# The last layer norm of a three-block transformer with tokens on partitions, its result transposed before it is scaled

## What is computed

```python
x = layer_norm(ALPHA * x + merged @ w_out[l], ln1_g[l], ln1_b[l])
u = causal_dwconv(x @ w_up[l], f_conv_w[l], f_conv_b[l])
u_gate, u_val = jnp.split(u, 2, -1)
x = layer_norm(ALPHA * x + (jax.nn.silu(u_gate) * u_val) @ w_down[l], ln2_g[l], ln2_b[l])
# layer_norm(x, g, b): (x - mean) * rsqrt(var + 1e-5) * g + b, over the 1024 features
```

## Time and profile before

| what | us |
|---|---|
| median of 3 runs (2580.94 to 2585.09) | 2582.67 |
| the profiled execution | 2586.92 |
| its span | 2585.1 |
| TensorE busy in it | 2513.1 |
| mean granted TensorE clock, share of full speed | 0.988 |

### The profile page before, as it was taken

The page is one execution under the profiler, slowest core; times in us unless marked ns, Lnnn a source line. Parts: engine busy times, 40 slices in busy tenths (PEclk is TensorE's granted clock), DMA queues, the critical chain, the costliest instruction groups (busy, mean ns, idle before and its releaser), DMA issues.

```text
span 2585.1 us, 30721 instructions
## 1 busy us (share of the span) xinstructions
PE 2513.1 (97%) x11112; PEld 1990.6 (77%) x11112; DVE 1369.7 (53%) x1916; ACT 667.3 (26%) x1101; POOL 1563.8 (60%) x1061
## 2 busy tenths in 40 slices
PE   7999999999999999999999999999999999999998
PEld 6875688888877776688867886867888777888876
DVE  5975683221379999968214426344356244534534
ACT  3006621100254434421022114133114121300102
POOL 2640257766779898667643765624764467666653
PEclk8999999999999999999999999999999999999999
DMA  9620132333222322122321231311332222233321
GB/s 298 222 94 1 52 123 86 98 98 98 98 82 82 97 73 74 53 98 96 105 76 33 98 98 46 103 49 53 98 94 66 65 82 93 70 98 98 89 96 47
DMA packets 224141, 231.46 MB, mean 90 GB/s; under 512 B 12219, under 2 KB 213788, under 8 KB 223900
## 3 DMA queue, kind: packets, MB, share of 16 engines
q1 hardware_dynamic: 221104, 229.33, 28.0%
q10 hardware_dynamic: 2924, 0.66, 0.1%
HBM read 227.87 MB, written 2.10 MB: 89 GB/s over the span
## 4 chain that ended last, share of the span: by engine, by line
PE 85%; DVE 8%; DVEq 2%; ACT 2%; POOLq 1%; issue 1%; POOL 1%; DMA 1%; ACTq 0%; SPq 0%
PE PS L1540 64%; PE PS L1487 7%; DVE PS L3076 3%; PE PS L1348 3%; PE PS L2136 1%; DVEq L3078 1%; PE PS L1007 1%; PE PS L2338 1%; PE PS L2355 1%; PE PS L2127 1%; DVE PS L3120 1%; PE PS L2723 1%; DMA spare<-in_ada_w 1%; POOLq L1457 1%; PE PS L1777 0%
## 5 line engine op out<-in xcount | busy, mean ns | idle before, releaser
L1461 POOL TENSOR_TENSOR Wl<-raw,Wh 128x512 fp32r<-128x512 f32 (+1 forms) x764 | 1035.2, 1386 | 28.1 <-issue 0.5
L1455 POOL TENSOR_SCALAR Wh<-raw 128x2048 fp32r<-128x2048 f32 (+1 forms) x195 | 367.6, 1886 | 808.9 <-issue 370.9
L1540 PE MATMUL PS<-Hh,Wh 128*128 128x512 f32 x1936 | 765.9, 396 | 29.3 <-POOL Wl L1461 20.9
L1540 PE MATMUL PS<-Hl,Wh 128*128 128x512 f32 x1936 | 758.7, 392 | 0.0
L1540 PE MATMUL PS<-Hh,Wl 128*128 128x512 f32 x1936 | 758.5, 392 | 0.0
L1540 PEld LDWEIGHTS PS<-Hh,Wh 128*128 128x128 f32 x1936 | 366.5, 189 | 116.0 <-POOL Wl L1461 20.3
L1540 PEld LDWEIGHTS PS<-Hl,Wh 128*128 128x128 f32 x1936 | 366.8, 189 | 78.0 <-issue 1.9
L1540 PEld LDWEIGHTS PS<-Hh,Wl 128*128 128x128 f32 x1936 | 366.3, 189 | 77.5
L1540 PE MATMUL PS<-Bh,Wh 128*128 128x512 f32 x640 | 249.4, 390 | 2.1 <-POOL Wl L1461 2.1
L1540 PE MATMUL PS<-Bh,Wl 128*128 128x512 f32 x640 | 249.0, 389 | 0.0
L1540 PE MATMUL PS<-Bl,Wh 128*128 128x512 f32 x640 | 249.0, 389 | 0.0
(11 more groups left out here) (497 smaller groups left out, 3091.7 us busy)
## 6 DMA issues: line engine op xcount, KB each, us to landing
raw<-in_w_in SPq DMA_DIRECT2D x44, 1024.0 KB, 5.4
raw<-in_w_ff SPq DMA_DIRECT2D x32, 1024.0 KB, 5.3
raw<-in_conv_w_in SPq DMA_DIRECT2D x24, 1024.0 KB, 5.2
raw<-in_ret_w_in SPq DMA_DIRECT2D x24, 1024.0 KB, 5.1
spare<-in_ada_w SPq DMA_DIRECT2D x20, 1024.0 KB, 8.9
raw<-in_w_up SPq DMA_DIRECT2D x20, 1024.0 KB, 5.3
raw<-in_w_out SPq DMA_DIRECT2D x8, 1024.0 KB, 4.9
raw<-in_conv_w_out SPq DMA_DIRECT2D x8, 1024.0 KB, 5.0
```

The source lines that it names most:

```text
L1455: pool.tensor_scalar(st.Wh[0:rows, slot, k, 0:cols], st.raw_slot(slot)[0:rows, k, 0:cols], 1.0, 1.0, ALU.mult, ALU.mult)
L1461: ins = pool.tensor_tensor(st.Wl[0:rows, slot, k, 0:cols], st.raw_slot(slot)[0:rows, k, 0:cols], st.Wh[0:rows, slot, k, 0:cols].bitcast(F3 ...
L1540: mm = pe.matmul(out, lhs, rhs, start=(k == parts[0][0] and n == 0), stop=(k == parts[-1][0] and n == 2))
```

## The change

`CentredNorm` for ln2 and `store_part` are replaced by one class, `LastNorm`. In short:

- **During down 2** (now one round of four phases): behind chunk k=3 of tile 2, TensorE transposes X chunks 0 to 3 as they are into banks 4 to 7. Tile 3 is multiplied one bank after the other (all of b=0, then all of b=1), with transposes of chunks 4, 5 in the first half and 6 in the second. VectorE takes `bn_stats` of these banks, which have tokens on partitions, so that a statistic is one number for each partition. It adds chunk 6 to X after the first bank.
- **After down 2:** chunk 7 is added, transposed and counted; `bn_aggr` gives mean and variance for each token; ScalarE has meanwhile made gain x X for each chunk (`scaled`), and TensorE turns these into banks of the result. The mean and the bias come into the same banks by one product for each bank: `spread` (columns with the mean and the standard deviation in high and low parts) times `factors` (rows with gain and bias). VectorE and ScalarE multiply by rstd on the way from PSUM, and four stores follow, one for each 128 tokens.
- **Between down 0 and up 1** stands a new part, `prepare`: VectorE clears the rows and the columns, SP waits for this and loads gain and bias as six rows (two DMAs of 12 KB), and VectorE rounds and splits them.
- The 18 small products before the transposes, the pivot and the sums of squares are gone.

```diff
+    def load_rows(self, sp):
+        sp.wait_ge(self.cleared, 1)
+        sp.dma_start(self.rows[0:3, :], self.gain_row.to_broadcast([3, D])).then_inc(self.rows_in, 16)
+        sp.dma_start(self.rows[3:6, :], self.bias_row.to_broadcast([3, D])).then_inc(self.rows_in, 16)
+
+    def make_rows(self, dve):
+        dve.wait_ge(*self.rows_free)
+        dve.memset(self.rows, 0.0)
+        dve.memset(self.columns.bitcast(F32), 0.0)
+        dve.tensor_tensor(self.low_row, self.st.ident[:, 1:2], self.st.ident[:, 4:5], ALU.add)
+        dve.drain().then_inc(self.cleared, 1)
+        dve.tensor_scalar(self.sign, self.low_row, -2.0, 1.0, ALU.mult, ALU.add)
+        dve.wait_ge(self.rows_in, 32)
+        dve.tensor_copy(self.rounded, self.rows)
+        dve.drain()
+        dve.tensor_scalar(self.rows, self.rows, self.low_row, None, ALU.mult)
+        dve.drain()
+        dve.scalar_tensor_tensor(self.factors, self.rounded.bitcast(F32), self.sign, self.rows, ALU.mult,
+                                 ALU.add).then_inc(self.rows_made, 1)
...
+    def within_bank(self, pe, p, b, k):
+        if (p, b, k) == (2, 0, 3):
+            self.raw(pe, (0, 1, 2, 3))
+        if (p, b, k) == (3, 0, 3):
+            self.raw(pe, (4, 5))
+        if (p, b, k) == (3, 1, 3):
+            self.raw(pe, (6,))
...
+    def counts_before_last(self, dve, i, p):
+        self.count(dve, 0)
+        dve.wait_ge(self.first_bank, 1)
+        self.add(dve, self.st.PS[:, 2 * self.own_slot(), :], 6).then_inc(self.seventh_in, 1)
+        self.count(dve, 1)
+        self.count(dve, 2)
...
+        pe.wait_ge(self.counted, NB)
+        turn_scaled(0, 0)
+        self.raw(pe, (7,))
+        for b in range(1, NB):
+            turn_scaled(b, 0)
+        pe.wait_ge(self.counted, 3 * NB)
+        for b in range(2):
+            turn_scaled(b, 1)
+        pe.wait_ge(self.columns_in, 1)
+        spread = st.PS[:, self.bank(3, 1), :]
+        for b in range(NB):
+            mm = pe.transpose(spread[:, b * P:(b + 1) * P], self.columns[:, b, :].bitcast(F32), st.ident)
+        mm.then_inc(self.columns_turned, 1)
+        turn_scaled(2, 1)
+        pe.wait_ge(self.rows_made, 1)
+        pe.wait_ge(self.columns_copied, 1)
+        add_means(0, 0)
+        add_means(0, 1)
+        turn_scaled(3, 1)
+        for b in range(1, NB):
+            add_means(b, 0)
+            add_means(b, 1)
...
+    def vector(self, dve):
+        st = self.st
+        self.count(dve, 3)
+        dve.drain()
+        for b in range(NB):
+            dve.bn_aggr(self.moments[:, b, :], self.counts[:, b, :, :].rearrange("p g n -> p (g n)"))
+        dve.drain().then_inc(self.var_in, 1)
+        dve.tensor_scalar(self.pair[:, :, 0], self.moments[:, :, 0], -1.0, None, ALU.mult)
+        dve.wait_ge(self.rstd_in, 1)
+        dve.scalar_tensor_tensor(self.pair[:, :, 1], self.moments[:, :, 1], self.eps, self.rstd, ALU.add, ALU.mult)
+        dve.drain()
+        for s in range(2):
+            dve.tensor_copy(self.columns[:, :, 3 * s:3 * s + 2],
+                            self.pair[:, :, s:s + 1].to_broadcast([P, NB, 2]))
+        dve.drain()
+        for s in range(2):
+            ins = dve.tensor_tensor(self.columns[:, :, 3 * s + 2], self.pair[:, :, s],
+                                    self.columns[:, :, 3 * s].bitcast(F32), ALU.subtract)
+        ins.then_inc(self.columns_in, 1)
+        for b in range(NB):
+            dve.wait_ge(self.filled, 2 * b + 1)
+            dve.tensor_scalar(self.Y[:, b, 0:4 * P], st.PS[:, self.bank(b, 0), :], self.rstd[:, b:b + 1], None,
+                              ALU.mult).then_inc(self.left_out, 1)
...
+        if g == n_groups - 1:
+            downs.append(Seg(wd, F, 1, [Phase(p * TW, dve=add) for p in range(4)], row0=g * D, rows=rows, ready=made))
...
-                p_b, w_out, ln1.part, *ffn, ln2.part,
-                store_part(nc, st, out, lambda c: (ln2.hi_in, c + 1))]
+                p_b, w_out, ln1.part, *ffn[:3], ln2.prepare, *ffn[3:], ln2.part]
```

More of the change, by code:

```diff
@@ L1513, in seg @@
                     if g.mode != "tokens" else [(b, TW) for b in range(NB)]
-                if g.mode == "tokens":
+                bank_by_bank = p in g.bank_by_bank
+                if g.mode == "tokens" or bank_by_bank:
                     order = [(k, rows, b, m) for b, m in blocks for k, rows in parts]
@@ L1541, in seg @@
                                        stop=(k == parts[-1][0] and n == 2))
+                    if bank_by_bank and b == 0 and k == parts[-1][0]:
+                        mm.then_inc(g.first_bank, 1)
                 mm.then_inc(multiplied, 1)
@@ L2898, in group_norm_parts @@
     return squares, part
[L2901 to L2912, removed]
-        for c in range(KC):
[L2914 to L2922, removed]
-        for b in range(NB):
[L2924 to L2945, removed]
@@ new lines, with __init__, x_in, own_slot @@
+class LastNorm:
+    def __init__(self, nc, st, t, out, seg, eps, gain, gain_row, bias_row, rows_free):
+        self.st, self.t, self.out, self.seg, self.eps, self.gain = st, t, out, seg, eps, gain
+        self.gain_row, self.bias_row, self.rows_free = gain_row, bias_row, rows_free
+        self.ctx = ExitStack()
+        (self.cleared, self.rows_in, self.rows_made, self.first_bank, self.seventh_in, self.turned, self.counted,
+         self.gained, self.var_in, self.rstd_in, self.columns_in, self.columns_turned, self.columns_copied,
+         self.filled, self.left_out, self.right_out, self.stored) = sems(
+            nc, self.ctx, "l2", "cleared rows_in rows_made first_bank seventh_in turned counted gained var rstd "
+                                "columns columns_turned columns_copied filled left_out right_out stored")
+        A = st.A
+        self.rows = A[:, 10:12, :].rearrange("p c n -> p (c n)")
+        self.rounded = st.early[:, 12:14, :].rearrange("p c n -> p (c n)")
+        self.factors = st.early[:, 14:16, :].rearrange("p c n -> p (c n)")
+        self.columns = st.late[:, 12, :].rearrange("p (b n) -> p b n", b=NB)
+        self.spread = st.late[:, 13, :].rearrange("p (b n) -> p b n", b=NB)
+        small = lambda a, n: A[:, 30, a:a + n]
+        self.counts = small(0, 96).rearrange("p (b g n) -> p b g n", b=NB, g=4)
+        self.moments = small(96, 8).rearrange("p (b n) -> p b n", n=2)
+        self.pair = small(104, 8).rearrange("p (b n) -> p b n", n=2)
+        self.log, self.rstd = small(112, 4), small(116, 4)
+        self.low_row, self.sign = small(120, 1), small(121, 1)
+        self.scaled = st.spare[:, 8:16, :]
+        self.Y = st.spare[:, 0:8, :].rearrange("p (b c) n -> p b (c n)", b=NB)
+        seg.bank_by_bank, seg.first_bank, seg.within_bank = (3,), self.first_bank, self.within_bank
+        seg.phases[2].more = self.counts_before_last
+        seg.phases[3].dve = self.last_chunk
+        self.prepare, self.part = Part(ExitStack()), Part(self.ctx)
+        self.prepare.sync(self.load_rows)
+        self.prepare.vector(self.make_rows)
+        self.part.tensor(self.tensor)
+        self.part.scalar(self.scalar)
+        self.part.vector(self.vector)
+        self.part.sync(self.sync)
+    def x_in(self, c):
+        return (self.seventh_in, 1) if c == 6 else (self.seg.posted, self.seg.posted_at(0, c // 2))
+    def own_slot(self):
+        return (self.seg.base + 3) % 2
+    def bank(self, b, half):
+        own, other = self.own_slot(), 1 - self.own_slot()
+        return 4 + b if half == 0 else (2 * other, 2 * other + 1, 2 * own, 2 * own + 1)[b]
+    def load_rows(self, sp):
[16 more added lines that the diff above has]
+                                 ALU.add).then_inc(self.rows_made, 1)
+    def turn(self, pe, out, c, b):
+        return pe.transpose(out, self.st.X[:, c, b * P:(b + 1) * P], self.st.ident)
+    def raw_bank(self, c, b):
+        PS = self.st.PS
+        at = lambda k, n: PS[:, k, n * P:(n + 1) * P]
+        if c < 4:
+            return at(4 + b, c)
+        if c < 6:
+            return at(self.bank(b // 2, 1), 2 * (b % 2) + c - 4)
+        return at(self.bank(2 + c - 6, 1), b)
+    def raw(self, pe, chunks_of):
+        for c in chunks_of:
+            pe.wait_ge(*self.x_in(c))
+            for b in range(NB):
+                mm = self.turn(pe, self.raw_bank(c, b), c, b)
+        mm.then_inc(self.turned, 1)
+    def within_bank(self, pe, p, b, k):
[5 more added lines that the diff above has]
+            self.raw(pe, (6,))
+    def count(self, dve, n):
+        dve.wait_ge(self.turned, n + 1)
+        PS = self.st.PS
+        for b in range(NB):
+            view = (PS[:, 4 + b, :], PS[:, self.bank(b // 2, 1), (b % 2) * 2 * P:(b % 2) * 2 * P + 2 * P],
+                    PS[:, self.bank(2, 1), b * P:(b + 1) * P], PS[:, self.bank(3, 1), b * P:(b + 1) * P])[n]
+            dve.bn_stats(self.counts[:, b, n, :], view).then_inc(self.counted, 1)
+    def add(self, dve, acc, c):
+        X = self.st.X[:, c, :]
+        return dve.scalar_tensor_tensor(X, X, 1.0, acc, ALU.mult, ALU.add)
```

(65 more changed lines are left out.)

3 lines of the change are left out of this document (added).

## The result

| | us, median | lowest to highest | runs |
|---|---|---|---|
| kernel before | 2582.95 | 2580.94 to 2586.09 | 5 |
| changed kernel | 2596.62 | 2593.32 to 2597.98 | 5 |

The ratio of all runs of the one to all runs of the other is 1.0047, with a 95% interval of 1.0035 to 1.0059: slower by 12 us (9 to 15). (The two medians lie 13.7 apart.) The forecast was +9.2, 2591.9, with a range of 2586.5 to 2597.5.

A forecast was written before the change was run, and what follows sets the result against it. TensorE, busy 97% of the span, was taken as the bound, with other engines on the path in the 27.6 us tail. 16.8 + 2.2 + 2.5 - 12.3 = +9.2 gave 2591.9 us, range 2586.5 to 2597.5.

The forecast's parts named there:

- Part 1, the queue: Between down 0 and up 1: SP's wait for `cleared` delays up 1's first load, idling TensorE; +16.8 us.
- Part 2, the clock: At the start of up 1: the granted clock falls inside TensorE's idle stretch and slows its first products; +2.2 us.
- Part 3, work within down 2: Within down 2: 28 transposes and a second entry of the 64-row chunk, less the pivot's product; +2.5 us.
- Part 4, the tail: From down 2's last product to the end: 15.3 us where it took 27.6; -12.3 us.
- Rival 4: Statistics around down 2's end cost twice the price, so VectorE ends tile 3: +13.4 us, 2596.1; chance 0.08.
- the row: Trace stretch 2570 to 2577 of the kernel before: almost only transposes, at clock 1.00; the forecast followed it.
- the rule that the prediction names: Trainium skill: transposes don't count as clock activity, so the tail's mean products may run slower; about 1 us longer.
- the late load would be hidden (1): SP's queue between down 0 and up 1: the load's reserve hides the delay; -9.8 us, 2572.9; chance 0.05.
- A longer landing through three transfers at once (3): Before up 1: row DMAs and two tiles' loads share the queue, first landing 2.7 later; +12.7, 2595.4; chance 0.12.
- Rival 2: No clear difference: small steps at their cheap ends, clock costs nothing; +3.7 to +5.1, 2586.4 to 2587.8; chance 0.13.

The follow-up runs named there:

- Experiments 1 and 6: Changed kernel with its row DMAs on ScalarE's queue: 0.9957, 2574.48; changed kernel with the rows' part cut in three, SP loading two segments later: 0.9960, 2574.73.
- experiment 2: The kernel before with only the rows' part between down 0 and up 1 (and its buffer) added, rows unused: ratio 1.0084, 2607.09.
- experiment 4: The changed kernel with 78 small products on TensorE between down 0 and up 1: ratio to the kernel before 1.0031, 2591.28.
- experiment 5: The changed kernel with 172 transposes of 128x128 on TensorE in the stall between down 0 and up 1: one run, 2592.47.
- experiment 3: The changed kernel with 70 small products on TensorE between down 0 and up 1: ratio to the kernel before 1.0045, 2595.16.
- experiment 7: The changed kernel with row DMAs on ScalarE's queue, plus 9 small products on TensorE ahead of down 1: ratio to the kernel before 0.9958, 2572.08.

## Why the prediction was right

The mechanism came as forecast in all four parts, and each was close to its size. By the trace the change costs +11.0, by all runs 12 (9 to 15), against the +9.2 of the sum. The last product of down 2 should come 21 to 22 us later than before; counted from the add of down 0 it comes 24.1 later (251.8 against 227.7). Part of the distance is a fall of the clock that wasn't forecast, and whether it belongs to the change is open. The measured 2596.62 lies inside the range but near its upper end, so the sum itself was short.

**Part 1, the queue: right, 0.6 us short.** `cleared` was forecast 3.3 us behind the start of the add and came at 3.3 (2325.17 to 2328.5); the load was issued at 4.4 (forecast 4.2); the split began 5.8 after that, where I had 5.3 (the median landing). Idle time 17.4 against 16.8. Experiments 1 and 6 take the wait off the queue in two ways and get the whole of it back, experiment 2 puts it into the other kernel and gets it all. The stall came once, as argued: the tiles behind it keep their 10.9.

**Part 2, the clock: right.** 2.2 forecast (the rows it was taken from give 2.3); 11 products in 4.73 us in the trace, 2.2 more than at 0.23 each, and 2.1 from first product to read recovered in experiment 4. What I didn't foresee is the second place where it falls, behind the 2.1 us wait at down 1, +1.6 in this trace. It is a term that the sum lacked: of the 1.8 between +9.2 and +11.0, parts 1 and 2 together have 0.9 (19.9 for 19.0), the dip has 1.6, part 3 has 0.2, and the tail takes 0.8 back. Experiment 2 has the stall without the dip and experiment 5 the dip without a stall, so it isn't shown to be an effect of the change.

**Part 3, work within down 2: right.** +2.7 for +2.5. The 28 transposes cost about what their rows said (3.1 us in the chain, for 2.9). The 16 in one piece took 1.66 in the timeline (2560.36 to 2562.02).

**Part 4, the tail: right, 0.8 too pessimistic.** 14.5 for 15.3. The unseen `bn_stats` has a duration like the reduction's, but four come in 2.49 us out of 512 columns (0.62 each), 1.42 out of 256 (0.36) and 0.89 out of 128 (0.22), where I took 0.69, 0.42 and 0.29. Rival 4, twice the price, is out. The first store is issued 7.6 after the last product, not 8.0, and from it to the end it took 6.9, not 7.3. (Up to the second drain the steps of the forecast add up to 3.8, at the full price of the aggregations, and not to the 3.6 written there; in the trace it is 3.1.)

**The clock and the transposes in the tail.** I went by the row and against the rule that the prediction names, and the mean products ran at the upper level: the granted clock is 1.00 in every microsecond from 2577 to 2586. Experiment 5 shows by itself that transposes hold it.

**The rivals.** That the late load would be hidden (1) is excluded by the 17.4 us. A longer landing through three transfers at once (3) has some truth: 0.5 of the 2.7 that I gave it. Rival 2 needed small steps at their cheap ends and a clock that costs nothing; the steps up to the load took 4.4 for 4.2, and the clock cost 2.

## What to carry to other kernels

A part that is put into the list of an in-order queue is charged for what stands behind its wait: ask how far ahead of the compute that queue runs (here 25 us), and if the event that it would wait for is newer than that, the prefetch is lost with every stage behind it. The cure does not take less work: the same two DMAs on an idle engine's queue, or later on the same queue, turned +0.47% into -0.43% and -0.40%. Both versions are ahead of both kernels, and can't be told apart from each other. Row statistics with tokens on partitions pay in a tail: 27.6 us became 14.5, with small operations of 0.1 to 0.3 us in place of 0.6 to 0.7 on 128x512, for 2.7 us more of TensorE's work ahead of it.

## What the runs showed that was not expected

- The granted clock can fall behind a wait of TensorE of only 2.1 us, and while real products run already: 0.66 over 2345 to 2350 in experiment 3, 0.88 and 0.78 at down 1 in the changed kernel. At the same wait at down 1 the kernel before kept 1.00. Where it fell there (three traces of nine), it cost 1.6 us each time.
- 172 fp32 transposes in a row, 0.11 us each, hold the clock at the upper level as 78 small products do.
- Traces of kernels with the same program up to down 0 reach it at 2323.7 to 2330.1, a spread of 6 us that has nothing to do with the change. Part of it is the clock: from 40 to 60 the mean granted clock is 0.63 in the trace of the kernel before and 0.77 in that of experiment 7, which has the earliest add; the rest wasn't traced. The median of a few runs carries this spread; the distance between two events in one trace doesn't.
